# Storing expert tiles by row number: the first layer's 32-slot output tiles go to DRAM through an indirect transfer

## The reference

```
def grouped_moe(h, router_w, router_bias, w_gate, w_up, w_down):
    scores = sigmoid(h @ router_w)                  # 16 experts in 4 groups
    ...                                             # best group, then the two best experts inside it
    gates = jnp.sum(jax.nn.one_hot(idx, N_EXPERTS) * w[..., None], axis=1)
    out = jnp.zeros_like(h)
    for e in range(N_EXPERTS):
        y = (jax.nn.silu(h @ w_gate[e]) * (h @ w_up[e])) @ w_down[e]
        out = out + gates[:, e:e + 1].astype(h.dtype) * y
    return out
```

## Time and profile before

| what | value |
|---|---|
| median of 3 runs | 962.0 us |
| the profiled execution | 957.07 us |
| its span in the trace | 955.3 us |
| PE, DVE, ACT, POOL busy | 807.3, 449.5, 265.1, 193.3 us |
| DMA, bytes moved | 309.03 MB, mean 324 GB/s |
| DMA queue q1 (SyncE's) | 275.78 MB, 73.1% of the span |
| DMA queue q0 (GpSimd's) | 30.22 MB, 8.8% of the span |

### The profile page before, as it was taken

The page is one execution under the profiler, slowest core; times in us unless marked ns, Lnnn a source line. Parts: engine busy times, 40 slices in busy tenths (PEclk is TensorE's granted clock), DMA queues, the critical chain, the costliest instruction groups (busy, mean ns, idle before and its releaser), DMA issues.

```text
span 955.3 us, 31672 instructions
## 1 busy us (share of the span) xinstructions
PE 807.3 (85%) x13340; PEld 542.0 (57%) x13341; DVE 449.5 (47%) x1101; ACT 265.1 (28%) x464; POOL 193.3 (20%) x365
## 2 busy tenths in 40 slices
PE   3799999999969898989888639999977785676895
PEld 2444444444458686868667525458445663565774
DVE  2379999944574344444333261665264221121232
ACT  2313536331412222222222130256032120111222
POOL 2300000010043334443424400000005121111220
PEclk9999999999979999999999959999998997787998
DMA  9992398568489999999999982881665999999992
GB/s 347 355 384 103 131 378 306 177 241 307 171 302 369 416 399 416 409 414 413 410 416 408 384 327 108 292 324 67 261 239 215 406 410 419 427 423 422 422 419 102
DMA packets 70694, 309.03 MB, mean 324 GB/s; under 512 B 9753, under 2 KB 10193, under 8 KB 54257
## 3 DMA queue, kind: packets, MB, share of 16 engines
q1 hardware_dynamic: 54608, 275.78, 73.1%
q0 software_dynamic: 15040, 30.22, 8.8%
q10 hardware_dynamic: 992, 2.26, 0.6%
HBM read 297.38 MB, written 14.20 MB: 326 GB/s over the span
## 4 chain that ended last, share of the span: by engine, by line
DMA 50%; PE 25%; DVE 18%; issue 3%; SPq 2%; ACT 2%; POOL 0%; DVEq 0%; POOLq 0%; ACTq 0%
DMA weight_ring<-in_exp_w_down 10%; DMA weight_ring<-in_exp_w_up 10%; DMA weight_ring<-in_exp_w_gate 10%; DVE arena L1069 9%; PE ps L609 7%; DMA arena<-in_exp_w_up 7%; DMA hT<-in_exp_w_down 5%; DMA arena<-in_exp_w_gate 4%; PE ps L875 3%; PE ps L832 3%; DMA weight_ring<-in_ev_w_in 2%; PE ps L575 2%; SPq L371 2%; PE ps L776 2%; PE ps L915 1%
## 5 line engine op out<-in xcount | busy, mean ns | idle before, releaser
L776 PE MATMUL ps<-weight_ring,arena 128*32 128x128 f32 x5760 | 185.6, 292 | 45.9 <-DMA weight_ring<-in_exp_w_up 28.1
L776 PEld LDWEIGHTS ps<-weight_ring,arena 128*32 128x32 f32 x5760 | 175.8, 119 | 60.0 <-DMA weight_ring<-in_exp_w_up 26.8
L1374 DVE TENSOR_TENSOR arena<-arena,ps 128x64 f32<-128x64 f32 x128 | 28.3, 221 | 228.4 <-ACT arena L1758 228.3
L1758 ACT ACTIVATE arena<-ps 128x64 f32<-128x64 f32 x128 | 28.7, 224 | 358.2 <-PE ps L776 358.2
L575 PE MATMUL ps<-hT,weight_ring 128*128 128x512 f32 x256 | 114.7, 604 | 2.4 <-DMA weight_ring<-in_ev_w_in 2.1
L1069 DVE SCALAR_TENSOR_TENSOR arena<-arena,par 128x512 f32<-128x512 f32 x132 | 94.8, 749 | 4.0 <-DVE arena L1100 0.8
L786 PE MATMUL ps<-weight_ring,arena 128*32 128x256 f32 x1440 | 92.6, 382 | 1.5 <-DMA weight_ring<-in_exp_w_down 0.9
L776 PE MATMUL ps<-arena 128*32 128x128 f32 x2432 | 75.2, 283 | 17.2 <-DMA arena<-in_exp_w_up 14.3
L575 PEld LDWEIGHTS ps<-hT,weight_ring 128*128 128x128 f32 x256 | 48.3, 192 | 66.8 <-issue 62.7
L776 PEld LDWEIGHTS ps<-arena 128*32 128x32 f32 x2432 | 72.0, 115 | 21.6 <-issue 19.2
L1758 ACT ACT_TABLE_LOAD x64 | 82.1, 1283 | 6.3 <-DVEq L1333 1.2
(11 more groups left out here) (324 smaller groups left out, 866.6 us busy)
## 6 DMA issues: line engine op xcount, KB each, us to landing
weight_ring<-in_ada_w SPq DMA_DIRECT2D x24, 2048.0 KB, 14.3
weight_ring<-in_exp_w_gate SPq DMA_DIRECT2D x22, 2048.0 KB, 10.0
weight_ring<-in_exp_w_up SPq DMA_DIRECT2D x22, 2048.0 KB, 10.4
weight_ring<-in_exp_w_down SPq DMA_DIRECT2D x22, 2048.0 KB, 10.9
arena<-in_exp_w_gate SPq DMA_DIRECT2D x10, 2048.0 KB
hT<-in_exp_w_down SPq DMA_DIRECT2D x10, 2048.0 KB, 11.1
arena<-in_exp_w_up SPq DMA_DIRECT2D x10, 2048.0 KB
weight_ring<-in_ev_w_in SPq DMA_DIRECT2D x4, 2048.0 KB, 19.6
```

The costliest lines, as they stand in the source:

```text
L776: last = mm(ps[32 * qd:32 * qd + 32, 1 + hh, 0:P].rearrange("p (m n) -> p m n", m=2), xgT[:, MT * k:MT * k + MT], w2[:, k, :, at:at + 64], ...
L1758: s.activation(act_sl[:, 64 * hh:64 * hh + 64], ps[:, 1 + hh, 0:64], ACT.Silu).then_inc(s_sl[l], 1)
```

## The change

Each store of layer 0 becomes an indirect transfer with a row number for each partition.

- GpSimd makes a table `place` at the start: for tile `g` and partition `32 q + s` the number `4 (32 g + s) + q` of the 1 KB quarter row in `y_rows`, less `BEYOND`.
- In layer 0's routing DVE multiplies it by 1 for a used slot and by 0 for an unused one, and adds `BEYOND` (two instructions, then `s_place`). So a used slot has its row number and an unused one has 8192, which is past the end of the 6656 quarter rows.
- In each tile step GpSimd copies a column of the table `sdst` to `scur` (a third small copy beside the two that were there), and the store is an `indirect_dma_start` with `bounds_check`, whose unused slots aren't moved.
- The fills now cover all 1664 rows of `y_rows` by four transfers where three covered the last 1152, and DVE waits for four.
- The second `s_const` goes out a little earlier at the start.

```
+BEYOND = float(4 * MT * 64)
...
-            dve.wait_ge(s_fill, 48)
+            dve.wait_ge(s_fill, 64)
...
                     v.tensor_scalar(slot_tab[:, :, 0], ps[:, 4, GMAX:2 * GMAX], CT - 0.5 - NOWHERE, None, ALU.is_lt)
+                    link(v.scalar_tensor_tensor(ids, ps[:, 4, GMAX:2 * GMAX], -0.5 * NOWHERE, place[:, :], ALU.is_lt, ALU.mult))
+                    v.tensor_scalar(sdst[:, :], ids, BEYOND, None, ALU.add).then_inc(s_place, 1)
...
+            pool.sem_inc(s_const, 1)
+            link(g.iota(place[:, :], [[4 * MT, GMAX]], base=-int(BEYOND), channel_multiplier=4, **kw))
+            link(g.tensor_scalar(pcol[:, 3:4], pcol[:, 2:3], -4.0 * P * NOWHERE, 1.0 - 4 * MT, ALU.add, ALU.mult))
+            link(g.tensor_scalar(place[:, :], place[:, :], pcol[:, 3:4], None, ALU.add))
             link(g.tensor_scalar(pcol[:, 3:4], pcol[:, 2:3], 0.25, -P * NOWHERE, ALU.mult, ALU.add))
-            pool.sem_inc(s_const, 1)
...
-            for i in range(3):
-                rows = y_dram[E * MT + TOK * i:min(E * MT + TOK * i + TOK, (MAXTILES + AHEAD) * MT), :]
+            for i in range(4):
+                rows = y_dram[TOK * i:min(TOK * i + TOK, (MAXTILES + AHEAD) * MT), :]
...
-                places = y_dram.rearrange("(g s) (q n) -> g q s n", s=MT, q=4)
+                places = y_dram.rearrange("s (q n) -> (s q) n", q=4)
...
                         g.tensor_copy(gcur[:, nxt:nxt + 1], gidx[:, bass.ds(k + (AHEAD + 1), 1)]).then_inc(s_gc[l], 1)
+                        if not l:
+                            g.tensor_copy(scur[:, u:u + 1], sdst[:, bass.ds(k, 1)]).then_inc(s_gc[l], 1)
                         pool.wait_ge(s_xg[l], k + 2)
-                        pool.wait_ge(s_gc[l], k + 1)
+                        pool.wait_ge(s_gc[l], (k + 1) * (2 - l))
...
-                            g.dma_start(places[k], y_sb[u]).then_inc(s_yo[u], 16)
+                            g.indirect_dma_start(places, bass.IndirectOffsetOnAxis(scur[:, u:u + 1], 0), y_sb[u], None,
+                                                 bounds_check=4 * MT * (MAXTILES + AHEAD) - 1, oob_is_err=False).then_inc(s_yo[u], 16)
...
+                if not l:
+                    pool.wait_ge(s_place, 1)
                 four_tiles(0)
```

More of the change, by code:

```diff
@@ L160, in build @@
         gates2 = sb("gates2", [P, 2, NT])
+        place = sb("place", [P, GMAX])
+        scur = sb("scur", [P, AHEAD], I32)
         gcur = sb("gcur", [P, AHEAD], I32)
@@ L205, in build @@
         slot_tab = reg(12288 + GMAX, 2 * GMAX).rearrange("p (g c) -> p g c", c=2)
+        sdst = reg(12288 + 3 * GMAX, GMAX).bitcast(I32)
         xg, xgT = reg(0, 256), reg(256, 256)
@@ L271, in build @@
         s_fill = sem("unused_rows_filled")
+        s_place = sem("store_index_ready")
         s_yfree = sem("tile_out_buffer_free")
```

## The result

| kernel | median of its runs | range |
|---|---|---|
| before | 962.0 us (7 runs) | 960.89 to 965.4 |
| changed | 972.12 us (7 runs) | 967.96 to 974.67 |

The ratio of the changed kernel to the kernel before is 1.0092, with a 95% interval of 1.0074 to 1.0109. I forecast 957.7 us, in a range from 954.0 to 963.2. The changed kernel is slower by 10 us, and the time is outside the range. The profiled execution took 974.67 us, its span is 972.8.

The account below looks back on a forecast made before the run. Weight transfers were taken to bound layer 0's expert stage. Bytes -2.4, small packets -2.2 and routing +0.3 sum to -4.3 us: profiled 952.8, median 957.7 us, range 954.0 to 963.2.

Parts of the forecast that it names:

- GpSimd's loop: Layer 0's tile steps: longer store issue and extra copy cost 0 us, covered by DVE's and PE's work.
- D: Rival: GpSimd's slow issue of scattered writes takes over the bound in the tile loop, 973 us; chance 0.06.
- 22.5 us: TensorE's idle time in 216 us of layer 0's expert stage; the tile loop lengthens it only beyond this.
- The base: Profiled execution of the kernel before, 957.07 us; the runs' median taken as 4.9 us above the profiled one.
- C: Rival: layer 0's expert stage reaches layer 1's transfer rate, -6.2 us, 955.8 us; chance 0.15.
- Small packets: Layer 0's stores: 3648 fewer small packets with the indirect store, -2.2 us, ends 0 and 3.0.
- Bytes: Layer 0's stores: unused slots skipped save 1.00 MB at 409 GB/s, -2.4 us, ends 0 and 2.6.
- Routing: Layer 0's routing: two more DVE instructions ahead of the gate weights, +0.3 us, ends 0 and 0.6.
- the fills: Start of the kernel: 2.1 MB more filled, landing before anything needs it, 0 us.
- the end of the stage: Layer 0's last store and first row gather: start moves by -0.6 to +0.3 us, taken as 0.
- E: Rival: the larger fills delay a needed weight chunk, +5.1 us, 962.8 us; chance 0.07.
- B: Rival: the indirect store keeps the direct one's 144 packets, or they cost nothing; only bytes remain, 959.9 us; chance 0.22.

Follow-up runs that it names:

- the control: Kernel before, unchanged, rerun beside the changed-store kernels on chip 15, without holds: median 957.1 us, ratio 0.9985.
- job 3: Chip 3, no holds, against the kernel before: changed kernel unchanged 0.9926, with all slots stored 0.9934, with no slot stored 0.9908.
- direct kernel: Changed kernel with its direct store back, all else kept, against the kernel before: 1.0003 on a chip with holds, 0.9986 on one without.
- the fills alone: Kernel before with only the four larger fills, against the kernel before: 1.0007, on a chip with holds.
- job 1: Chip 7, with holds, against the kernel before: direct store back 1.0003, unused semaphore 1.0001, larger fills 1.0007, two unused tiles 0.9998.
- late store: Changed kernel with tile k - 1's store issued in step k ahead of the gather, against the kernel before: 0.9936 without holds, 1.0466 with.

## Why the prediction was wrong, by its own steps

**GpSimd's loop, 0 us.** This is the step that failed. Its numbers were right: the issue takes 1.02 us, and no transpose of line 1216 waits for bring. What it left out is that TensorE can stand still beside an indirect issue on GpSimd. I asked who waits for GpSimd in program order, and TensorE doesn't. On the chips that hold, the term is 38 x 0.6 = 23 us of TensorE's time, where I had 0. I gave the only way in which the tile loop would take the bound over a chance of 0.06 (D, by a slow issue), and that way was the wrong one.

The 22.5 us that I named as the point from which the tile loop decides was too high as well. Only 10.7 us of TensorE's idle time were waits for weights. Another 10.7 us stood in the four waits for "issue", which the changed kernel without holds has as well (12.3 us). By my own sum 23 us less 22.5 and less the 4.3 saved would have left the time as it was or shorter. The stage's tiles took 15.6 us more. The sign that I had put down for "wrong", DMA share under 1 with TensorE idle, came: 0.97.

The Trainium skill would have supported the 0 in SBUF — State Buffer, section Who interferes with whom: only the port pair that VectorE and GpSimd share causes contention, and TensorE's ports are its own. The trace of chip 3 agrees with that, with 124 loads in one piece. Those of chips 7, 12 and 14 don't, with gaps of 0.3 to 0.6 us; whether a port of the SBUF is what is fought for there, no run tells.

**The base.** The profile from which every term was read came out at 957.07 us, 3.8 us below the fastest of the three runs. I added the difference to the end as a constant. It was the trace's only hint of the two kinds of chip: it has no hold, like the 957.1 us of the control on chip 15, and the median of 962.0 is like the chips that hold. A sum made on one can't stand for the other, because the change adds indirect issues.

**The other terms, on the chips that don't hold.** There the forecast of -4.3 us was right in sign and mechanism, and too small. The measured ratios of 0.9926 and 0.9937 are -7.1 and -6.0 us, the size of C's -6.2.

- Small packets, -2.2: too low. The kernel that stores all slots indirectly moves the same bytes, and 0.9934 is -6.3 us against 0.9986, -1.3, with the direct store on another such chip. To the last tile, line 1405, it gains 4.0 us on the control of its own chip (533.21 against 537.22). In job 3's trace of it the engines move 422 GB/s between 378 and 512 us with 2117 packets in GpSimd's queue, the control 413 with 4034. I had set the upper end at 3.0, from the part of the small packets that is the stores', and the rate of layer 1, which I had also worked out as 4.6 us over the stage, was nearer.
  The 10.5 ns for a small packet in the Trainium skill (DMA: Bandwidth & Descriptors, section Bandwidth) gives 2.4 us as an estimate. The runs don't agree: with 4.0 to 5.0 us for 38 x 96 / 16 = 228 packets of each engine the runs give 18 to 22 ns.
- Bytes, -2.4: probably too high. The bytes themselves are as I counted: GpSimd's queue moves 32.26 MB with all slots, 31.22 with the used ones and 27.04 with none. In job 3 the changed kernel's last tile comes at 532.24 us, 0.9 us before the one with all slots (533.12). With no slot stored 4.2 MB more are left out. At my 409 GB/s that is 10.3 us. The ratios fall by 0.0018 and 0.0041 in the same jobs, 1.7 and 3.9 us, and the last tile comes 5.7 us earlier (526.21 against 531.88). By this a stored byte beside the weights costs a sixth to a half of its share. But with no slot stored little but the four fixed waits is left between the tiles, so these numbers are a lower end, and the ratios 0.9926 and 0.9934 of job 3 can't be told apart.
- Routing, the fills and the end of the stage, together 0.3: nothing speaks against it. The direct kernel has 1.0003 and 0.9986, the fills alone 1.0007 with 1.0020 at the upper end, 1.9 us. E, 5.1 us, is out.
- Written bytes: I expected 15.25 MB, and the page has 16.30 with all slots, with the used ones and with none. It doesn't count down for what is passed over, so it can't be used for this. The queue's own bytes above can.

**B, C.** B is out by the packets. C's rate was reached: 421 GB/s.

**What stays open.** In each of the six jobs all profiles are of one kind, and the changed kernel's times on the two kinds don't overlap (967.96 to 974.67 us, and 949.16 to 953.31). So indirect issues hold TensorE in some jobs and not in others. Whether it is the chip isn't shown, since no chip ran two jobs. The first comparison has both kinds in it, the profile of before without holds and the other with them, and the record doesn't say on which chips the two were taken. The cause isn't shown either: the kernels, the instruction counts and the issue's duration are the same on both, and nothing in a trace tells how the chips differ. Why the down product runs on beside a gather of layer 0 on a chip that holds is left open too, but the traces make it small: in job 1 its loads end at 353.97 us, 0.99 us after the start of the gather's issue, about where a hold would begin, and the next product's begin 0.19 us later. And no kernel here beats the one before on both kinds: on the chips that don't hold the changed kernel (0.9926 and 0.9937) is as fast as any complete one, with the late store (0.9936) and all slots stored (0.9934) beside it, and on those that do the direct store is (1.0003).

## What to carry to other kernels

An indirect transfer on GpSimd can cost TensorE about 0.6 us when its issue falls beside a streaming product, and 1.8 us for two in a row, although no semaphore joins them, so count issues as well as bytes and look for gaps in the weight loads that wait for "issue". When the profiled time lies outside the runs' own range, find out why before adding terms to it; and when a result contradicts a code-independent part of the trace, run the old kernel unchanged beside the new one, on more than one chip. Idle time of an engine is room for a delay only where it waits for what the change makes faster, so split it by what ended it before using it as a bound. Moving a wait in an engine's queue moves what stood behind it to an earlier time, so a place worked out from the old timeline is wrong.

## What the runs showed of the hardware

- In jobs on three named chips (7, 12, 14) an indirect issue of 1.0 us on GpSimd stopped TensorE's weight loads for 0.3 to 0.6 us, from 0.7 to 1.0 us after its start to 0.2 to 0.35 us after its end. In jobs on three others (0, 3, 15) the same instruction left the loads without a gap, beside all 39 stores of the changed kernel. A direct issue of 0.76 us stopped nothing on either.
- It does so when the store moves none of the tile (ratio 1.0108).
- During two issues in a row ScalarE saw TensorE's finished product 2.3 us late; during five, VectorE waited 3.9 us for one.
- An indirect store of 128 KB made 48 packets where the direct one made 144, and the stage's rate rose from 413 to 421 GB/s.
